# A hybrid decoder layer on one core: the first V unit of token tile 1 moves from VectorE to TensorE, and one-hot rows from VectorE to ScalarE

## What is computed

```python
def _peer(h, w_query, sub_keys, expert_u, expert_v):
    ...
    eid = i1 * N_KEYS + i2            # 128 x 128 experts
    g = jax.nn.softmax(best_s, axis=-1)
    ...
    a = jax.nn.gelu(jnp.einsum('td,thkd->thk', hx, expert_u[e]))
    return jnp.einsum('thk,thkd->td', gw * a, expert_v[e])
...
x = _layernorm(ALPHA * h + _peer(h, ...), ln2_g, ln2_b)
```

## Time and profile before

| | us |
|---|---|
| median of 3 runs (1780.84 to 1786.48) | 1783.23 |
| the profiled execution | 1784.41 |
| its span | 1782.6 |
| end of the last dot | 1386.6 |
| first `add_row` | 1413.1 |
| first matmul of the dense blocks (L945) | 1416.3 |
| first `add_row` that waits for its gather | 1472.6 |
| last that does | 1637.1 |

### The profile page before, as it was taken

How to read it: one execution, slowest core, us unless ns; L and a number is a source line. 1 busy time by engine, 2 the same in 40 slices (tenths; PEclk the granted TensorE clock), 3 DMA queues, 4 the chain that set the end, 5 groups by cost and what they waited for, 6 DMA issues and landing times.

```text
span 1782.6 us, 16637 instructions
## 1 busy us (share of the span) xinstructions
PE 1462.4 (82%) x6028; PEld 931.5 (52%) x6028; DVE 1400.2 (79%) x1940; ACT 384.3 (22%) x804; POOL 982.6 (55%) x591
## 2 busy tenths in 40 slices
PE   8999999999979708877767777788976899999900
PEld 7988999988668503333323333344536644444400
DVE  6666646676879998876788888677879797788998
ACT  5665464664101212102010102011111200000000
POOL 3210000000456677878776777888883187678881
PEclk9999999999989858989998899999995599999955
DMA  9876444474999999999999999999999399999994
GB/s 313 281 258 206 118 143 142 142 243 162 382 374 420 382 425 403 415 426 425 418 424 425 420 413 424 422 416 424 416 424 421 136 375 401 407 396 417 342 365 159
DMA packets 159810, 610.85 MB, mean 343 GB/s; under 512 B 21514, under 2 KB 74854, under 8 KB 97814
## 3 DMA queue, kind: packets, MB, share of 16 engines
q0 software_dynamic: 79232, 480.80, 66.5%
q1 hardware_dynamic: 80496, 128.99, 20.5%
HBM read 683.42 MB, written 2.10 MB: 385 GB/s over the span
## 4 chain that ended last, share of the span: by engine, by line
PE 26%; POOL 24%; DVE 18%; DMA 14%; issue 14%; DVEq 3%; ACT 1%; SPq 0%; POOLq 0%; ACTq 0%
PE psum_all L586 13%; POOL u_slot L524 13%; POOL v_slot L541 11%; DMA v_slot<-in_expert_v_dram,eid 10%; DVE xh L1778 6%; DVE u_slot L1743 6%; PE psum_all L726 4%; DMA u_slot<-in_expert_u_dram,eid 4%; DVEq L1770 1%; PE psum_all L751 1%; PE psum_all L707 1%; PE psum_all L611 1%; PE psum_all L613 1%; PE psum_all L937 1%; PE psum_all L962 1%
## 5 line engine op out<-in xcount | busy, mean ns | idle before, releaser
L1743 DVE SCALAR_TENSOR_TENSOR u_slot<-u_slot,xh 128x2048 f32<-128x2048 f32 x256 | 577.8, 2288 | 124.0 <-DMA u_slot<-in_expert_u_dram,eid 121.4
L962 PE MATMUL psum_all<-v_slot,diag 128*128 128x512 f32 x1024 | 509.2, 651 | 165.9 <-DMA v_slot<-in_expert_v_dram,eid 120.5
L524 POOL DMA_INDIRECT u_slot<-in_expert_u_dram,eid x256 | 446.2, 1743 | 282.1 <-DVE u_slot L1743 115.4
L541 POOL DMA_INDIRECT v_slot<-in_expert_v_dram,eid x240 | 466.2, 1942 | 150.8 <-DVEq L1779 81.9
L962 PEld LDWEIGHTS psum_all<-v_slot,diag 128*128 128x128 f32 x1024 | 204.1, 207 | 457.7 <-issue 235.6
L1778 DVE SCALAR_TENSOR_TENSOR xh<-v_slot,gate,xh 128x2048 f32<-128x2048 f32 x128 | 301.0, 2352 | 44.2 <-DMA v_slot<-in_expert_v_dram,eid 32.5
L1361 DVE TENSOR_TENSOR w_lo<-w_ring,w_hi 128x512 fp32r<-128x512 f32 x240 | 156.6, 688 | 77.6 <-ACT w_hi L1000 74.5
L586 PE MATMUL psum_all<-act_hi,w_hi 128*128 128x256 f32 x640 | 185.2, 289 | 1.3 <-DVE w_lo L1361 1.2
L586 PE MATMUL psum_all<-act_lo,w_hi 128*128 128x256 f32 x640 | 181.0, 283 | 0.0
L586 PE MATMUL psum_all<-act_hi,w_lo 128*128 128x256 f32 x640 | 180.4, 282 | 0.0
L1000 ACT ACTIVATE w_hi<-w_ring 128x512 fp32r<-128x512 f32 x240 | 139.4, 622 | 42.2 <-PE psum_all L586 42.0
(11 more groups left out here) (280 smaller groups left out, 1453.6 us busy)
## 6 DMA issues: line engine op xcount, KB each, us to landing
w_ring<-in_w_in_dram SPq DMA_DIRECT2D x88, 512.0 KB, 5.2
u_slot<-in_expert_v_dram SPq DMA_DIRECT2D x40, 1024.0 KB, 8.8
wo_ring<-in_w_out_dram SPq DMA_DIRECT2D x32, 512.0 KB, 5.5
wq_ring<-in_w_query_dram SPq DMA_DIRECT2D x32, 512.0 KB, 9.6
w_ring<-in_cmp_k_w_dram POOLq DMA_DIRECT2D x16, 512.0 KB, 5.9
w_ring<-in_cmp_v_w_dram POOLq DMA_DIRECT2D x16, 512.0 KB, 4.6
u_slot<-in_expert_u_dram,eid POOLq DMA_INDIRECT x256
v_slot<-in_expert_v_dram,eid POOLq DMA_INDIRECT x256
```

What stands on the lines that cost most here:

```text
L524: nc.gpsimd.indirect_dma_start(out=u_slot[m % RU][:, :], out_offset=None, in_=expert_u[0], in_offset=bass.IndirectOffsetOnAxis(ap=eid[:, n ...
L541: nc.gpsimd.indirect_dma_start(out=v_slot[m % RV][:, :], out_offset=None, in_=expert_v[0], in_offset=src, bounds_check=ROWS - 1, oob_is_er ...
L962: ins = nc.tensor.matmul(bank[4 + q][:, :], diag[:, n % 2, k, :], v_slot[m % RV][:, 512 * q:512 * q + 512], start=(m == 0), stop=False)
L1743: V.scalar_tensor_tensor(u_slot[m % RU][:, :], u_slot[m % RU][:, :], 1.0, xh[:, n // PH, :], ALU.mult, ALU.mult, accum_out=u_dot[:, n, k:k ...
```

## The change

It does five things that belong together.

1. Picks 128 to 143 (unit 8, the first V unit of tile 1) are summed by PE like those of tile 0, into banks 0 to 3. DVE has 112 `add_row` left instead of 128. V0_PICKS = 128 and PE_PICKS = 144 take the place of HALF_U.
2. Tile 0's sums leave their banks for a while: after pick 127 and the residual, ACT copies banks 4 to 7 to `sum0`, and PE puts them back with 4 identity matmuls (L984 of the changed kernel) before the dense blocks. In between banks 4, 5 and 6 serve tile 1's groups and transposes.
3. The one-hots of the second key are made by ACT (`key_rows`): for each of the 8 tokens Abs(iota - key), then one Relu(1 - x) over all 1024 columns. L1768 goes from DVE. `picks_out` becomes three copies, the key negated.
4. Tile 1's groups are spread: 8 stand between dots 244 and 254, one for every one or two dots, and on PE one before each of the picks 133 to 140; the other 8 come after. In tile 0, PE's groups start at pick 97 instead of 94.
5. The dense blocks have RD = 6 slots instead of 8; the rows `ln2g_sb` and `ln2b_sb` take the other two and are loaded after the blocks instead of before. POOL sends U picks up to 64 + (m + 1) * 4 / 3. Tile 0's norm is done in two operations of 2048 columns instead of eight of 512, and stored at once.

```diff
-HOT1_AT = 15 * TOPK + 5
+HOT1_AT = {15 * TOPK + 4 + 3 * b // 2: b for b in range(NG_T // 2)}
@@ PE
-            if m >= 94 and m % 2 == 0 and m < 94 + 2 * NG_T:
-                dense_rows(0, (m - 94) // 2)
+            if m >= 97 and m % 2 and m < V0_PICKS:
+                dense_rows(0, (m - 97) // 2)
+            if m == V0_PICKS:
+                for q in range(4):
+                    ins = nc.tensor.matmul(bank[4 + q][:, :], ident_a[:, :], xh[:, 0, 512 * q:512 * q + 512],
+                                           start=False, stop=True)
+                ins.then_inc(S["t0_part"], 1)
+                pe.wait_ge(S["dense_ok"], NG_T)
+            if m == V0_PICKS + 4:
+                pe.wait_ge(S["part_ok"], 1)
+                pick_transposes(1)
+            if V0_PICKS + 5 <= m < V0_PICKS + 5 + NG_T // 2:
+                dense_rows(1, m - V0_PICKS - 5)
@@ ACT
+        def key_rows(t, b):
+            g, n = NG_T * t + b, PICKS[t]
+            if g >= 2:
+                act.wait_ge(S["dense_mm"], g - 1)
+            for i in range(G_TOK):
+                nc.scalar.activation(hot2[0:n, g % 2, i, :], iota_key[0:n, :], ACT.Abs,
+                                     bias=pickT[0:n, t, 1, G_TOK * b + i:G_TOK * b + i + 1])
+            act.drain()
+            nc.scalar.activation(hot2[0:n, g % 2, :, :], hot2[0:n, g % 2, :, :], ACT.Relu, bias=one_col[0:n, :], scale=-1.0
+                                 ).then_inc(S["key_ok"], 1)
...
         unit(14)
+        expo_gate(15)
         picks_out(1)
         for b in range(NG_T):
-            if b == 11:
-                unit(15)
+            if b == NG_T // 2:
+                gelu_unit(15)
+            if b == 0:
+                key_rows(1, 0)
+            if b + 1 < NG_T:
+                key_rows(1, b + 1)
             dense_out(1, b)
@@ DVE
-        gates_of(NU - 1)
-        for b in range(TOPK * NU - HOT1_AT, NG_T):
+        for b in range(NG_T // 2, NG_T):
             hot_rows(1, b)
         V.tensor_scalar(xh[:, 1, :], xh[:, 1, :], ALPHA, None, ALU.mult)
         dve.drain()
-        for m in range(HALF_U, TOPK * NU):
+        for m in range(PE_PICKS, TOPK * NU):
+            if m == PE_PICKS + TOPK:
+                gates_of(NU - 1)
```

More of the change, by code:

```diff
@@ L320, in build @@
     s_v = [nc.alloc_semaphore(f"s_v{i}") for i in range(RV)]
-    s_d = [nc.alloc_semaphore(f"s_d{i}") for i in range(RU)]
+    s_d = [nc.alloc_semaphore(f"s_d{i}") for i in range(RD)]
     def bview(i, *shape):
@@ L418, in _ @@
                 load_wq(j, q)
-        sp.wait_ge(S["v_used"], HALF_U)
+        for f in range(FD):
+            if f < RD:
+                sp.wait_ge(S["dots_done"], TOPK * NU - RU + f + 1)
+            else:
+                sp.wait_ge(S["dense_used"], f - RD + 1)
+            first = ROWS + NKEY * f
+            sp.dma_start(u_slot[f % RD][:, :], expert_v[0][first:first + NKEY, :]).then_inc(s_d[f % RD], 16)
         for row, src in ((ln2g_sb, ln2_g), (ln2b_sb, ln2_b)):
@@ L944, in dense_mm @@
             for q in range(4):
-                ins = nc.tensor.matmul(bank[(4 if t == 0 else 0) + q][:, :], src, u_slot[f % RU][:, 512 * q:512 * q + 512],
-                                       start=(t == 1 and f == 0), stop=(f == FD - 1))
+                ins = nc.tensor.matmul(bank[(4 if t == 0 else 0) + q][:, :], src, u_slot[f % RD][:, 512 * q:512 * q + 512],
+                                       start=False, stop=(f == FD - 1))
                 if f == FD - 1:
                     ins.then_inc(S[("t0_sum", "t1_sum")[t]], 1)
-            if t and f < FD - RU:
+            if t and f < FD - RD:
                 ins.then_inc(S["dense_used"], 1)
-        for m in range(HALF_U):
+        for m in range(PE_PICKS):
             n, k = divmod(m, TOPK)
@@ L1338, in _ @@
                 unit(11 + b // 6)
+            if b == 10:
+                diagonals(8)
+            if b == 0:
+                key_rows(0, 0)
+            if b + 1 < NG_T:
+                key_rows(0, b + 1)
             dense_out(0, b)
+        act.wait_ge(S["t0_part"], 1)
+        for q in range(4):
+            ins = nc.scalar.activation(sum0[:, 512 * q:512 * q + 512], bank[4 + q][:, :], ACT.Copy)
+        ins.then_inc(S["part_ok"], 1)
         unit(14)
+        expo_gate(15)
         picks_out(1)
         for b in range(NG_T):
-            if b == 11:
-                unit(15)
+            if b == NG_T // 2:
+                gelu_unit(15)
+            if b == 0:
+                key_rows(1, 0)
+            if b + 1 < NG_T:
+                key_rows(1, b + 1)
             dense_out(1, b)
@@ L1764, in hot_rows @@
                 dve.wait_ge(S["dense_mm"], g - 1)
-            row, key, coef = (pickT[0:n, t, i, cols].unsqueeze(2) for i in range(3))
+            row, coef = (pickT[0:n, t, i, cols].unsqueeze(2) for i in (0, 2))
             V.tensor_tensor(hot1[0:n, g % 2, :, :], iota_row[0:n, :].unsqueeze(1).to_broadcast([n, G_TOK, FD]),
                             row.to_broadcast([n, G_TOK, FD]), ALU.is_equal)
-            V.tensor_tensor(hot2[0:n, g % 2, :, :], iota_key[0:n, :].unsqueeze(1).to_broadcast([n, G_TOK, NKEY]),
-                            key.to_broadcast([n, G_TOK, NKEY]), ALU.is_equal)
             dve.drain()
@@ L1791, in norm_out @@
             dve.drain()
-            for q in range(4):
-                cols = slice(512 * q, 512 * q + 512)
-                V.scalar_tensor_tensor(dst[:, cols], src(q), l2mv[:, t, 0:1], ln2g_sb[:, cols], ALU.subtract, ALU.mult)
-                dve.drain()
-                V.scalar_tensor_tensor(dst[:, cols], dst[:, cols], l2rs[:, t:t + 1], ln2b_sb[:, cols], ALU.mult, ALU.add
-                                       ).then_inc(S["final_ok"], 1)
-        def right_cols(q):
-            return xh[:, 1, 512 * q:512 * q + 512]
         V.memset(eps2[:, :], LN_EPS).then_inc(S["eps2_ok"], 1)
@@ L1826, in _ @@
                     hot_rows(0, HOT0_AT[m])
-                if m >= HOT1_AT:
-                    hot_rows(1, m - HOT1_AT)
-        gates_of(NU - 1)
-        for b in range(TOPK * NU - HOT1_AT, NG_T):
+                if m in HOT1_AT:
+                    hot_rows(1, HOT1_AT[m])
+        for b in range(NG_T // 2, NG_T):
             hot_rows(1, b)
@@ L1849, in _ @@
         for q in range(4):
-            V.bn_stats(l2st[:, 1, q, :], right_cols(q))
+            V.bn_stats(l2st[:, 1, q, :], xh[:, 1, 512 * q:512 * q + 512])
         stats_of(1)
-        norm_out(1, right_cols, xh[:, 1, :])
+        root_inverse(1)
+        for q in range(4):
+            cols = slice(512 * q, 512 * q + 512)
+            V.scalar_tensor_tensor(xh[:, 1, cols], xh[:, 1, cols], l2mv[:, 1, 0:1], ln2g_sb[:, cols], ALU.subtract, ALU.mult)
+            dve.drain()
+            V.scalar_tensor_tensor(xh[:, 1, cols], xh[:, 1, cols], l2rs[:, 1:2], ln2b_sb[:, cols], ALU.mult, ALU.add
+                                   ).then_inc(S["final_ok"], 1)
     block_cm.__exit__(None, None, None)
```

88 lines of the change are left out of this document (45 added, 43 removed).

## The result

| | before | after | forecast |
|---|---|---|---|
| median, 12 runs each | 1783.51 us | 1789.54 us | 1768.0 |
| ratio of the medians, 95% interval | | 1.0033, 1.0026 to 1.0041 | 0.991 |
| span of the profiled execution | 1782.6 | 1785.8 | 1767.4 |
| end of the last dot | 1386.6 | 1407.2 | 1396 |
| first `add_row` | 1413.1 | 1446.1 | 1434.4 |

The change loses 6.0 us by the medians (3.2 by the spans) where I forecast a gain of 15. The time lies in the range given (1750 to 1790), the direction was wrong. `add_row` begins 33.0 us later instead of 21.3, and has 39.5 us less to do, as forecast; it then waits 11.6 us more.

The account below looks back on a forecast made before the run. Gathers bound until the last dot, then DVE's chain of adds sets the end. Contended stretch to 1679.8, plus 62.2 for remaining picks, 23.7 beside adds and 1.7 for norm rows: 1767.4 span, 1768.0 us forecast; range 1750 to 1790.

Parts of the forecast that it names:

- The last dot: End of tile 1's dots: DMA, full until about 1392, bounds them; last dot at 1396 against 1386.6 before.
- my lower bound: For the last dot: 1386 if all dense loads yield to the gathers.
- Rival C: Before the adds: dense loads yield, last dot 1388, PE one pick behind, adds from 1417, end 1750; chance 0.14.
- The upper bound: For the last dot: 1402 if V picks beyond 143 squeeze in among the gathers.
- Unit 8 ends behind the last dot, +13: On PE, group 7 and picks 140 to 143 stand behind dot 254, so unit 8 ends 13 us after the last dot.
- From the last dot to the adds, +38.4: ACT's keys bound most late groups, 4.36 us each; adds start at 1434.4, dense blocks at +49.3, 1445.3.
- Sixteen adds less: On DVE: 16 adds fewer at 2.47 us save 39.5 us, called certain.
- The contended stretch: Where adds share DMA with dense loads: from 1501.5 to 1679.8, 178.3 us, 59.6 picks at 2.99 us.
- The norm rows at the end: Loaded behind all dense blocks, the two norm rows cost the gathers 1.7 us.
- Other covers: Dense loads issued 13.7 us ahead, slowest took 11.2; PE's sums at 1711.7, before DVE reaches pick 246 at 1717.
- Rival A: In unit 8, PE waits for one-hots and falls to the lower clock; about half of 70 us, end 1797; chance 0.14.
- Rival B: Before the adds: sixteen V picks, 28.6 us, eat the gain; last dot 1405, adds 1449, end 1783; chance 0.15.

Follow-up runs that it names:

- hold: The changed kernel, but none of the first six dense blocks is loaded before the last dot: 1776.27 us, span 1775.0.
- both: The changed kernel with the edits of `hold` and `shift` together: 1766.95 us, span 1764.3.
- shift: The changed kernel, but PE's first eight groups of tile 1 stand before picks 136 to 143 instead of 133 to 140: 1776.74 us, span 1775.0.
- keysdve: The changed kernel, but the second key's one-hots are made by VectorE again instead of ScalarE: 1786.24 us, span 1784.5.
- bothrows: `both`, with the two norm rows loaded right behind the first six dense loads instead of behind all 40 blocks: 1761.70 us, span 1760.5.
- nounit: The changed kernel, but unit 8 is added by VectorE as before (128 adds), with all 16 groups behind tile 0's picks: 1778.10 us, span 1775.7.

## Why the prediction was wrong, step by step

The sum ended at 1767.4 and the span is 1785.8, a miss of 18.4 us. `hold`, the changed kernel with one delay removed, splits it: its last dot is at 1394.5 (forecast 1396), its adds start at 1434.1 (1434.4), its dense blocks at 1445.6 (1445.3), and it ends at 1775.0. So 10.8 us arise before the adds and 7.6 behind them.

- **The last dot failed, 1396 against 1407.2.** I counted megabytes: V picks, 5.5 dense loads, a DMA that is full until 1392. The step that failed is the full DMA, and with it the reading that an early issue is an early landing. In the run DMA stood at 0.93 over 107.2 us, where it was 1.01 before. The difference is 8.6 us of the 11.2 missed, an estimate from these shares. Early issue did not help: four of the six loads were issued behind the last U gather and still landed in 8 to 10 us beside it; without all six (`hold`) the last dot comes 12.7 us sooner.
- **That `hold` meets 1396 is luck.** The sum had 5.5 loads in front of the last dot, and `hold` has none there. It should have come at 1386, my lower bound "if all dense loads yield to the gathers", and came at 1394.5:

```profile
1300.00:1394.50 94.50, 76.28 (x255) 41.34 (x253) 61.72 (x73) 43.32 (x111) 63.88 (x35) 0.87 0.91 363
```

A share of 0.91 is 0.10 below the kernel before; over 94.5 us that is 9.5 us, an estimate, and about the 8.5 by which the bound fails. Rival C, which had the last dot at 1388 with the loads yielding, is refuted with it. So the count was too low with the loads (11.2) and without (8.5). Why DMA is not full there stays open. It is not POOL's waiting for PE alone: in `both` these waits, from 1300 to the last dot, are 17.2 us instead of 20.0, the share is 0.94, and the last dot does not move (1394.5). The upper bound, 1402 "if V picks beyond 143 squeeze in", named an intruder of which `shift` shows nothing.
- **Unit 8 ends behind the last dot, +13: right (+14.9),** and I booked it as given. `shift` shows that it is a choice of order worth 10.8 us. I had the cause in hand (group 7 and picks 140 to 143 behind dot 254) and left it out of the rivals but for C's "one pick behind".
- **From the last dot to the adds, +38.4: right (+38.9); to the dense blocks, +49.3: right (+50.6).** Errors cancel in it: the group's pace was 4.03 instead of 4.36, the lag of unit 8 was 1.9 more, and putting the sums back took 5.1 us (1452.69 to 1457.77) where I had 3.5. The rule of the Trainium skill, "ScalarE: Activation LUTs", section Rules for kernel authors, by which the prediction had an estimate of 5.2 a group, gives too much here: eight Abs took 2.40 us, as the earlier trace rows said, and not 3.3; for the Relu of 1024 columns, 1.15 us, it fits. Its advice, VectorE for such work, is right by 1 to 3 us (`keysdve`).
- **Sixteen adds less, 39.5 us: right.** 18 + 76 + 18 adds.
- **The contended stretch failed: 178.3 us and 59.6 adds forecast, 227.1 and 76 measured.** Its rate, 2.99 us an add, was right. I carried both its ends over from the kernel before, 56.2 us after the start of the dense blocks and 220.8 + 13.7. In the run the first wait came 33.8 us after that start and the last 260.8. `hold`, from its first wait to its last, `add_row` alone:

```profile
1477.40:1707.80 230.40, 181.22 (x77) 1.00 1.00 408
```

These are 77 - 59.6 = 17.4 more adds at 2.99 instead of 2.47, 9.0 us; less the 1.7 that I had booked for the norm rows it is 7.3, and the miss behind the adds' start is 7.6. Of it the norm rows are 3.8 (`bothrows`) less that 1.7. The late end does not come with unit 8: `nounit`, with 128 adds, has its last wait 261.0 us after its dense blocks start. It came with the rest of the change, of which six slots instead of eight and the rows at the end bear on DMA; no run prices the slots. Why the first wait comes sooner is open: DMA moved only 250 GB/s in the stretch ahead of it, where it was 325.
- **The norm rows at the end: mis-sized.** They were booked at 1.7 us, and in a full DMA they cost 3.8 (`bothrows`).
- **Other covers held.** Dense loads landed in 7.9 to 10.4 us against 13.7. No wait stands at pick 246.
- **Small slips of the sum** change nothing: 276.7 us are 40 blocks at 6.92, not 40.3 at 6.87, and the terms of ACT's 3.65 add up to 3.55, or 3.75 with the whole drain (in the run 3.6).
- **Rival A** (PE at the lower clock in unit 8, 1797) came true in small. After a wait of PE for one-hots the next group took 3.64 instead of 1.88 and the next pick about 5 instead of 3.7: with the picks behind other waits of PE it was two groups and five picks, some 12 us of PE, most of it off the chain to the adds. On the chain to the adds lie one such group and one such pick, 3.4 us, where the rival needed 21 to be slower by itself. The PE rows below, of the changed kernel and then of `both`, show the pair.

```profile
1397.85 3.64 PE L941 MATMUL psum_all<-hot,hot 112*128 112x40 f32 x16 [6.10 <-DVE hot L1811]
1401.28 5.33 PE L977 MATMUL psum_all<-v_slot,diag 128*128 128x512 f32 x8
```

```profile
1385.59 1.88 PE L941 MATMUL psum_all<-hot,hot 112*128 112x40 f32 x16
1387.29 3.68 PE L977 MATMUL psum_all<-v_slot,diag 128*128 128x512 f32 x8
```

From 1300 to the last dot the granted clock is 0.84 in the changed kernel, 0.87 in `hold`, 0.88 in `shift` and 0.92 in `both`, in which PE no longer waits for one-hots there. So a part of what the two edits win can be the clock's; no run prices it.
- **Rival B** (the gathers eat the gain, 1783) was the nearest: last dot 1405 and adds 1449 against 1407.2 and 1446.1. It was right on the state and, as its reason, named V picks 144 to 150 and all dense loads landing first. The loads are shown by `hold`; of the picks `shift` shows nothing. It missed the longer contended stretch, which is why it had 1783 and not 1786. I gave it 0.15 because POOL issues those picks behind the last U pick. For the picks that held; the loads stand in another queue.
- **`both` came out at 1767, the forecast's number,** but by other means: two errors of 18.4 in all, against two gains of 21.5 that the change as written does not have.
